# State-space step sizes from raw fp32 weights, in four quarters of a bank

## What is computed

```
proj = h @ w_in                                   # ..., dt_raw: 32 columns, ...
dt = softplus(dt_raw + dt_bias)                   # (tokens, 32)
a = -exp(a_log)
acs = cumsum(dt * a)                              # within each chunk of tokens
y_t = sum over s <= t of (C_t . B_s) exp(acs_t - acs_s) dt_s x_s
```

## Time and profile before

| | |
|---|---|
| median of 3 runs | 1696.14 us (1695.81 to 1696.51) |
| the profiled execution's own time | 1696.76 us |
| its span | 1694.7 us |
| TensorE busy | 1682.7 us, 99% of the span |
| VectorE, ScalarE, POOL busy | 874.8, 706.2, 792.7 us |
| mean granted TensorE clock | 0.998 of full speed |
| share of the chain that ended last | TensorE 97% |

### The profile page before, as it was taken

How to read it: one execution, slowest core, us unless ns; L and a number is a source line. 1 busy time by engine, 2 the same in 40 slices (tenths; PEclk the granted TensorE clock), 3 DMA queues, 4 the chain that set the end, 5 groups by cost and what they waited for, 6 DMA issues and landing times.

```text
span 1694.7 us, 21862 instructions
## 1 busy us (share of the span) xinstructions
PE 1682.7 (99%) x7957; PEld 1371.5 (81%) x7957; DVE 874.8 (52%) x1365; ACT 706.2 (42%) x977; POOL 792.7 (47%) x605
## 2 busy tenths in 40 slices
PE   9999999999999999999999999999999999999998
PEld 7777778788888888788878888788888888888887
DVE  6334474563616167797897878863355511101113
ACT  5333354431323134456464554784424422222232
POOL 1433354445545455543434344444545544654453
PEclk9999999999999999999999999999999999999999
DMA  5222222274636342233222332222222222332232
GB/s 187 91 84 74 74 96 90 75 261 161 229 118 216 124 155 99 96 106 125 100 100 101 118 103 99 100 75 100 75 99 100 76 98 99 129 128 91 99 124 100
DMA packets 32539, 193.82 MB, mean 114 GB/s; under 512 B 3648, under 2 KB 5696, under 8 KB 13792
## 3 DMA queue, kind: packets, MB, share of 16 engines
q1 hardware_dynamic: 25376, 158.89, 26.8%
q10 hardware_dynamic: 7104, 34.15, 6.0%
HBM read 190.86 MB, written 2.16 MB: 114 GB/s over the span
## 4 chain that ended last, share of the span: by engine, by line
PE 97%; DVE 1%; POOL 1%; DMA 1%; ACT 0%; SPq 0%; issue 0%; DVEq 0%; POOLq 0%
PE gemm_bank L511 25%; PE gemm_bank L504 25%; PE gemm_bank L505 25%; PE gemm_bank L542 4%; PE gemm_bank L558 4%; PE gemm_bank L551 3%; PE gemm_bank L546 1%; PE gemm_bank L789 1%; PE aux_bank L975 1%; PE aux_bank L655 1%; PE aux_bank L980 1%; PE aux_bank L960 1%; POOL h L482 1%; PE aux_bank L681 1%; DMA w_raw<-weights_dram 1%; PE aux_bank L672 1%
## 5 line engine op out<-in xcount | busy, mean ns | idle before, releaser
L454 POOL TENSOR_TENSOR w_lo<-w_raw,w_hi 128x512 fp32r<-128x512 f32 x580 | 771.2, 1361 | 881.8 <-ACT w_hi L1259 870.6
L504 PE MATMUL gemm_bank<-a_hi,w_hi 128*128 128x512 f32 x1008 | 402.6, 399 | 0.0
L505 PE MATMUL gemm_bank<-a_lo,w_hi 128*128 128x512 f32 x1008 | 393.2, 390 | 0.0
L1259 ACT ACTIVATE w_hi<-w_raw 128x2048 fp32r<-128x2048 f32 x145 | 276.5, 1907 | 187.0 <-PE gemm_bank L511 122.7
L504 PE MATMUL gemm_bank<-b_hi,w_hi 128*128 128x512 f32 x688 | 267.8, 389 | 0.0
L505 PE MATMUL gemm_bank<-b_lo,w_hi 128*128 128x512 f32 x688 | 267.6, 389 | 0.0
L511 PE MATMUL gemm_bank<-a_hi,w_lo 128*128 128x512 f32 x1024 | 258.6, 395 | 0.0
L511 PEld LDWEIGHTS gemm_bank<-a_hi,w_lo 128*128 128x128 f32 x1024 | 190.2, 188 | 44.9 <-issue 6.2
L504 PEld LDWEIGHTS gemm_bank<-a_hi,w_hi 128*128 128x128 f32 x1008 | 189.3, 188 | 43.9 <-issue 5.6
L505 PEld LDWEIGHTS gemm_bank<-a_lo,w_hi 128*128 128x128 f32 x1008 | 189.5, 188 | 39.4 <-issue 1.9
L2161 DVE SCALAR_TENSOR_TENSOR aux_bank<-scratch,gcol,aux_bank 128x511 f32<-128x511 f32 (+15 forms) x240 | 165.8, 734 | 14.2 <-ACT aux_bank L1485 11.9
(11 more groups left out here) (414 smaller groups left out, 2127.7 us busy)
## 6 DMA issues: line engine op xcount, KB each, us to landing
w_raw<-weights_dram SPq DMA_DIRECT2D x146, 1024.0 KB, 4.8
arena<-ada_dram ACTq DMA_DIRECT2D x32, 768.0 KB, 4.4
acc<-cum_rows ACTq DMA_DIRECT2D x8, 512.0 KB, 3.9
h<-x_t_dram SPq DMA_DIRECT2D x8, 256.0 KB, 6.2
row_b<-cum_rows ACTq DMA_DIRECT2D x4, 512.0 KB, 4.8
scratch<-cum_rows ACTq DMA_DIRECT2D x4, 512.0 KB, 4.3
out_t_dram<-a_raw SPq DMA_DIRECT2D x7, 256.0 KB, 2.2
w_raw<-weights_dram SPq DMA_DIRECT2D x4, 256.0 KB, 5.3
```

The source lines that it names most:

```text
L454: ins = pool.tensor_tensor(wlo[s][:, w], raw[s][:, w], whi[s][:, w].bitcast(F32), ALU.subtract)
L504: pe.matmul(gemm_bank[bank][:, :], whi[slot][:, w], hi[:, k, :], start=(n == 0), stop=False)
L505: pe.matmul(gemm_bank[bank][:, :], whi[slot][:, w], lo[:, k, :], start=False, stop=False)
L1259: act.activation(whi[panel % 2][:, :], raw[panel % 2][:, :], ACT.Copy).then_inc(w_hi_ready, 1)
```

## The change

The dt tile is no longer made of three rounded products per chunk. POOL copies the 32 columns of each chunk of the raw panel to `w_dt`. TensorE multiplies them as fp32, 128 x 32 weights by 512 columns, on a_hi and on a_lo, both read as fp32. Four chunks go to four quarters of the bank (partitions 0 to 31, 32 to 63, ...): chunks 0 to 3 after the a_hi chunk 3, chunks 4 to 7 after the a_hi chunk 7, and likewise on a_lo. So each quarter holds the sum over two chunks. The bias is added in the first quarter (it is zero elsewhere), and `dt_x` has 128 partitions. `turn_steps` multiplies it by `head_sum`, a 128 x 32 matrix of four identities below one another that POOL makes from `ident`; this adds the quarters and turns them at once. The pair's products on a_hi and a_lo are as before.

`turn_steps` is moved behind the high products of tile 2 of the group, and the low products of tiles 2 and 3 follow the high ones of both. ScalarE rounds panel P_DT + 2 right after the a_hi chunks, instead of after the dt tile; it waits for a signal on the last filler, the last reader of the panel buffer `whi[0]`.

```diff
@@ -168,7 +168,7 @@
         seg_pair = scratch[:, 14:16, :]
         ln_sum = b_n
         x_win = [seg_pair[:, 0, :], seg_pair[:, 1, :], state[:, 2, :]]
-        dt_x = scratch[0:SSM_HEADS, 4, :]
+        dt_x = scratch[:, 4, :]
         dt_e, dt_s, dt_q = [scratch[:, 2, c * P:(c + 1) * P] for c in range(3)]
         dt_r, dt_p = [aux[3][:, c * P:(c + 1) * P] for c in range(1, 3)]
         da_t = scratch[:, 3, 0:P]
@@ -194,6 +194,8 @@
         shift_out = new_part[:, 0:2]
         rinv2 = sb("rinv2", [P, QT])
         one_gain2 = sb("one_gain2", [P, 2])
+        head_sum = sb("head_sum", [P, 2 * SSM_HEADS])
+        w_dt = arena[:, 26, 0:KC * SSM_HEADS].rearrange("p (k n) -> p k n", k=KC)
         group_inv = sb("group_inv", [P, GROUPS * QT])
         group_root = sb("group_root", [P, GROUPS * QT])
         sq = sb("sq", [P, 2, S])
@@ -301,6 +303,8 @@
         cum_stored = sem("cum_stored")
         row_loaded = [sem(f"row_loaded{s}") for s in range(3)]
         dtt_done = sem("dtt_done")
+        dt_prepared = sem("dt_prepared")
+        wide_done = sem("wide_done")
         cumt_ready = sem("cumt_ready")
         last_done = sem("last_done")
         cross_step = sem("cross_step")
@@ -473,6 +477,14 @@
             pool.wait_ge(a_lo_ready, 3 * KC)
             low_parts(P_MLP // 2, 1, (1, 2, 3))
             panels_of(P_MLP // 2 + 1, P_DT // 2)
+            pool.wait_ge(w_loaded[0], 16 * (P_DT // 2) + 16)
+            pool.tensor_copy(w_dt[:, :, :], raw[0][:, :].rearrange("p (k n) -> p k n", k=KC)[:, :, 0:SSM_HEADS]) \
+                .then_inc(dt_prepared, 1)
+            pool.tensor_tensor(head_sum[:, :], ident[:, 0:2 * SSM_HEADS], ident[:, 2 * SSM_HEADS:4 * SSM_HEADS], ALU.add) \
+                .then_inc(dt_prepared, 1)
+            pool.wait_ge(dt_prepared, 2)
+            pool.tensor_tensor(head_sum[:, 0:SSM_HEADS], head_sum[:, 0:SSM_HEADS], head_sum[:, SSM_HEADS:2 * SSM_HEADS],
+                               ALU.add).then_inc(dt_prepared, 1)
             low_parts(P_DT // 2, 0)
             low_parts(P_DT // 2, 1, (0, 1), (first_half, 1))
             pool.wait_ge(w_hi_ready, P_GRP + 1)
@@ -878,39 +890,58 @@
                                start=True, stop=True)
             mm.then_inc(r_ready, 1)
 
+            def dt_products(operand, chunks, start=False, stop=False):
+
+                for g, k in enumerate(chunks):
+                    mm = pe.matmul(gemm_bank[T_DT % 4][g * SSM_HEADS:(g + 1) * SSM_HEADS, :],
+                                   w_dt[:, k, :], operand[:, k, :].bitcast(F32), start=start, stop=stop)
+                return mm
+
             def first_three():
 
-                three = [(P_DT, T_DT, 0), (P_GRP, T_GRP, 0), (P_GRP, T_GRP + 1, 1)]
+                pair = [(T_GRP + j, j) for j in range(2)]
                 for k in range(KC):
                     pe.wait_ge(a_hi_ready, 3 * KC + k + 1)
-                    for panel, t, j in three:
+                    for t, j in pair:
                         w = slice((2 * k + j) * P, (2 * k + j + 1) * P)
                         if k == 0:
-                            pe.wait_ge(w_hi_ready, panel + 1)
+                            pe.wait_ge(w_hi_ready, P_GRP + 1)
                             pe.wait_ge(bank_free[t % 4], t // 4 + 1)
-                        pe.matmul(gemm_bank[t % 4][:, :], whi[panel % 2][:, w], a_hi[:, k, :], start=(k == 0), stop=False)
+                        pe.matmul(gemm_bank[t % 4][:, :], whi[P_GRP % 2][:, w], a_hi[:, k, :], start=(k == 0), stop=False)
                         if k == 0:
-                            pe.wait_ge(w_lo_ready, panel + 1)
-                        pe.matmul(gemm_bank[t % 4][:, :], wlo[panel % 2][:, w], a_hi[:, k, :], start=False, stop=False)
-                for tiles in (three[:1], three[1:]):
-                    for k in range(KC):
-                        pe.wait_ge(a_lo_ready, 3 * KC + k + 1)
-                        for panel, t, j in tiles:
-                            w = slice((2 * k + j) * P, (2 * k + j + 1) * P)
-                            mm = pe.matmul(gemm_bank[t % 4][:, :], whi[panel % 2][:, w], a_lo[:, k, :],
-                                           start=False, stop=(k == KC - 1))
-                            if k == KC - 1:
-                                mm.then_inc(tile_done, 1)
-
-            keep_wide(7)
+                            pe.wait_ge(w_lo_ready, P_GRP + 1)
+                        pe.matmul(gemm_bank[t % 4][:, :], wlo[P_GRP % 2][:, w], a_hi[:, k, :], start=False, stop=False)
+                    if k == 3:
+                        pe.wait_ge(dt_prepared, 1)
+                        pe.wait_ge(bank_free[T_DT % 4], T_DT // 4 + 1)
+                    if k % 4 == 3:
+                        dt_products(a_hi, range(k - 3, k + 1), start=(k == 3))
+                for k in range(KC):
+                    pe.wait_ge(a_lo_ready, 3 * KC + k + 1)
+                    if k == 3:
+                        dt_products(a_lo, range(0, 4))
+                    if k == KC - 1:
+                        dt_products(a_lo, range(4, KC), stop=True).then_inc(tile_done, 1)
+                    for t, j in pair:
+                        w = slice((2 * k + j) * P, (2 * k + j + 1) * P)
+                        mm = pe.matmul(gemm_bank[t % 4][:, :], whi[P_GRP % 2][:, w], a_lo[:, k, :],
+                                       start=False, stop=(k == KC - 1))
+                        if k == KC - 1:
+                            mm.then_inc(tile_done, 1)
+
+            keep_wide(6)
+            pe.matmul(gemm_bank[MIX_SPARE][:, :], whi[P_DT % 2][:, 0:P], whi[P_DT % 2][:, 0:S], start=True, stop=True) \
+                .then_inc(wide_done, 1)
             first_three()
             ident_h = ident[0:SSM_HEADS, 0:SSM_HEADS]
 
             def turn_steps():
 
                 pe.wait_ge(bank_free[T_DT % 4], free_value(T_DT))
+                pe.wait_ge(dt_prepared, 3)
                 for c in range(QT):
-                    pe.transpose(aux[2][:, c * SSM_HEADS:(c + 1) * SSM_HEADS], dt_x[:, c * P:(c + 1) * P], ident_h)
+                    pe.matmul(aux[2][:, c * SSM_HEADS:(c + 1) * SSM_HEADS], dt_x[:, c * P:(c + 1) * P],
+                              head_sum[:, 0:SSM_HEADS], start=True, stop=True)
                 pe.wait_ge(decay_ready, 1)
                 pe.matmul(aux[3][:, 0:SSM_HEADS], neg_exp_a[:, 0:1].to_broadcast([SSM_HEADS, P]), ident_h,
                           start=True, stop=True).then_inc(dtt_done, 1)
@@ -982,8 +1013,13 @@
                     mm.then_inc(y_done, 2)
 
                 if first:
-                    turn_steps()
-                    g(2), g(3)
+                    blocks = [[(2 * k + j, k) for k in range(KC)] for j in range(2)]
+                    for j in range(2):
+                        tile_high(0, P_GRP + 1, T_GRP + 2 + j, 8, 16, blocks[j], a_hi, a_lo, first=(j == 0))
+                        if j == 0:
+                            turn_steps()
+                    for j in range(2):
+                        tile_low(0, P_GRP + 1, T_GRP + 2 + j, 8, blocks[j], a_hi, first=(j == 0))
                     running_sums()
                 else:
                     g(0), g(1), g(2), g(3)
@@ -1441,14 +1477,14 @@
 
             act.wait_ge(mod_ready, MLP_GROUPS)
             operand_shifted(2, 0)
+            act.wait_ge(wide_done, 1)
+            round_weights(0, P_DT + 2, 0, 0, 0)
 
 
             act.activation(neg_exp_a[:, :], cols[0:SSM_HEADS, COLS["a_log"]:COLS["a_log"] + 1], ACT.Exp) \
                 .then_inc(decay_ready, 1)
             act.wait_ge(tile_done, T_DT + 1)
-            act.activation(dt_x, gemm_bank[T_DT % 4][0:SSM_HEADS, :], ACT.Identity,
-                           bias=cols[0:SSM_HEADS, COLS["dt_bias"]:COLS["dt_bias"] + 1]).then_inc(bank_free[T_DT % 4], 1)
-            round_weights(0, P_DT + 2, 0, T_DT + 1, 0)
+            act.activation(dt_x, gemm_bank[T_DT % 4][:, :], ACT.Identity, bias=col("dt_bias", 0)).then_inc(bank_free[T_DT % 4], 1)
 
             def exp_steps():
                 act.wait_ge(dtt_done, 1)
```

## The result

| | before | after |
|---|---|---|
| median | 1696.14 us (1695.76 to 1696.84, 22 runs) | 1698.61 us (1698.12 to 1699.00, 22 runs) |
| span of the profiled execution | 1694.7 us | 1696.8 us |

The changed kernel takes 1.0014 times as long, with a 95% interval of 1.0008 to 1.0020: 2.5 us more, inside what was set beforehand as no difference (0.2%), though its interval leaves out 1. 5.44 us of TensorE's products were taken out, yet the kernel got longer.

A forecast was written before the change was run, and what follows sets the result against it. TensorE, busy 1682.7 of 1694.7 us, was taken as the bound. Terms -5.44 + 4.88 + 1.2 + 0.6 + 0.85, less 0.75 of old waits, gave +1.3; with +0.6 behind the stage, +1.9: 1698.0 us, range 1695.0 to 1702.3.

The forecast's parts named there:

- the likeliest case: Whole kernel: the forecast itself, 1697 to 1699.4 us, likeliest 1698.0; chance 0.54.
- step 6: Behind the stage: softplus chain starts 5.0 us later, DVE 2.4 late relative to TensorE, +0.6 us of new waits.
- 1 and 2: Stage: the dt tile's 24 products removed, 5.44 us; four fp32 visits of 1.22 us added, 4.88.
- A: Visits: the quarters run one behind another, 2.55 us more in each visit, giving 1707.4 us; chance 0.08.
- B: Visits: each quarter waits for its neighbour's second record, +1.27 us a visit, giving 1702.2 us; chance 0.05.
- 3: Products on a_hi: TensorE now waits for chunks 1 to 3, 1.2 us that the removed products had covered.
- 4: Next panel rounded sooner: POOL's subtractions stretch three a_lo to 1.7 us each; TensorE waits 0.85 us, bounds 0 to 2.
- 5: Turning of dt: 1.27 us plus 0.1 on return, +0.6 net; its waits are covered by the tile ahead.
- Rival C: First group: DVE becomes the bound, its lateness passing 1.8 to 2.2 us of slack, giving 1700.7 us; chance 0.08.
- D: Cheap case: subtractions don't hold a_lo, switching half hidden, DVE makes its deadlines; about -0.2, 1695.9 us; chance 0.22.
- E: Thin stream between 680 and 685: clock falls to half again, losing 1.7 us, giving 1699.7; chance 0.03.

The follow-up runs named there:

- one_quarter: Changed kernel with all dt products sent to one quarter of the columns, one behind another: 1709.01 us, ratio 1.0076 to the kernel before.
- filled: both_waits with panel 58 rounded ahead of the a_hi chunks, tile 2 as third tile beside each chunk, its a_lo products ahead of the turning: 1696.42 us.
- turn_first: Changed kernel with the turning back ahead of the group's tiles 2 and 3, each tile's low products behind its own high ones: 1697.87 us.
- copies_sooner: Changed kernel with VectorE copying the first group's head columns ahead of its first short convolution instead of behind it: 1697.19 us.
- both_waits: Changed kernel with POOL starting panel 58's low parts only after the last a_lo, and head columns copied ahead of the first short convolution: 1696.80 us.
- best: filled with the four visits to the quarters merged to two and the turning right behind the pair: 1695.86 us, ratio 0.9997 to the kernel before.

## Why the prediction was right, and where not

The time came out at 1698.61, 0.6 us over the 1698.0 and within the likeliest case. Steps 1 to 5 held as mechanisms and nearly as sizes; step 6 came near by luck in part, as told there. By the prediction's steps:

1 and 2, products and visits: right. A visit was put at 1.22 with its switches; from the start at 684.10 to the return of the full pace at 685.76, less two full products of 0.23, it is 1.20. The first records of all four quarters start between 684.43 and 684.45, the second ones from 684.88 to 684.90, as the prediction's sign of being right asked. Rivals A and B are refuted: all eight records of a visit end within 1.06 us, where B needs five times 0.43, and one_quarter shows what A's serial order costs (3.55 us). The weight loads of the first visit, in the same trace:

```profile
684.42 0.16 PEld L896 LDWEIGHTS gemm_bank<-a_hi,arena 128*32 128x32 f32 x8 [0.37 <-issue]
```

The Trainium skill ("TensorE: Matmul & The Clock Gate", Part 3: Packing small matmuls) says that weight loads overlap running products only where the row group differs. These rows don't bear it out: the products take all 128 rows, and all eight loads are over by 684.58, while the second records start at 684.88 only. The same page ("Why this matters for your kernels") says that products on separate column groups run at the same time, and the rows of after agree with that for fp32 and four groups.

3, the supply of a_hi: right. Chunk 3 was to be ready 3.89 us after the first product; it came at 683.28, 3.89 after. The filled kernel got 0.62 of this stage's waits back, so they were real.

4, the rounding moved ahead: mechanism right. Three a_lo were to take 1.7 us each and the last to end 16.15 after the first product; it ended at 695.53, 16.14 after. TensorE's wait was 0.58 and not 0.85, because it came to the last visit 0.2 later than walked through. Taking the clash out gave back 0.60. That rounding sooner gains nothing on TensorE was not tested, and the rows speak against it. In its old place the rounding stands behind dt_x, and the dt tile now ends later: dt_x ended at 697.41 in after, so with its 1.90 us the rounding would have ended at 699.3 at the soonest (an estimate from these two rows), and TensorE asked for the panel at 697.15. So the early rounding cost 0.6 in the clash, and may have saved some 2 us.

5, the turning: right, 1.27 against 1.24 (700.79 to 702.03). Uncovered by a tile ahead it was to lose 0.8; turn_first, which uncovers it, loses 0.44.

Sum to the running sums: +1.3 predicted, +1.22 measured.

6, VectorE's lateness: this is the step that was mis-sized. It had +0.6 in two waits "near 740 and 761"; measured is one wait of +1.41 at 740.61, and none at 762. Two errors stood against each other, and that the sum came near is in part their doing: without the clash the time would have been some 1.0 over before, as in copies_sooner, where +1.9 was forecast. The first error is the lateness relative to TensorE, 1.96 and not 2.4, which alone would have cost nothing. The second is that the prediction took back the 0.9 of a step that no longer meets POOL, but did not ask what VectorE would newly meet when it is late. The rows for it stood in the trace of before: the four copies of 0.17 us, and POOL's next burst 0.79 us behind their end. So did the price of such a meeting, in one more copy, of 98 columns, which takes 0.20 us at its other places and 0.85 at the first, inside POOL's burst:

```profile
L2166 DVE COPY gcol<-cols x4: 199/202/852, 705.3 to 998.7; 128x98 f32<-128x98 f32 x2, 128x98 f32 x2
```

(This row gives the shortest, the median and the longest of the four in ns.) Rival C had the right place and the right direction, a deadline missed past 2.2 us of slack. The measured wait of 1.41 lies between the 0.6 of the forecast and C's 3.3.

D failed on all its three conditions: a_lo did meet POOL, a visit cost its 1.20 in full, and VectorE missed a deadline. E is refuted. The window over the thin stream in after (columns as in the earlier trace rows) shows the clock granted in full, 1.00 of 2.4 GHz.

```profile
679.40:684.40 5.00, 4.72 (x16) 2.69 (x16) 5.00 (x9) 2.75 (x4) 5.00 (x5) 1.00 0.25 103
```

Where the 5.44 us went, then: four visits took 4.8, the uncovered a_hi supply and the bigger turning ate what was left and 0.6 more, a_lo's clash 0.6, and the copies' clash 1.4. The last two are accidents of order, and both_waits removes them. The first three are the change itself, which without accidents is still 0.59 us longer than before in the trace and 0.57 in the medians, though the interval of both_waits includes no difference. Only new work in the opened gaps (filled) and fewer visits (best) bring it level.

## What to carry to other kernels

Products taken off TensorE count only where its operands are already there; where a supply paces it, removing work opens gaps, and one must bring other work to stand in them. When a step makes an engine later, compare its new times with the bursts of the engine whose port it shares, down to its smallest instructions: slack computed from its own work alone is too large. Measuring from an event in the stage instead of from the start of the execution lets one trace account for tenths of a microsecond.

## What the runs showed of the hardware

Four fp32 products of 32 weight columns and 512 columns of data, in four column quarters, take nearly the time of one: 0.99 us to the next start, 1.85 for eight, and 3.55 for four in one quarter, 0.89 each. Two switches can be read beside that: 0.10 going into the narrow form (684.10 to 684.43, where a full product takes 0.23), and 0.11 between the first full product behind it and the second (685.42 to 685.76).

A copy of 128x32 fp32 from SBUF to SBUF takes 0.17 us alone, and up to 1.27 beside POOL in after. The stretched ones end at 726.15 and 727.43, where POOL's first two of four subtractions end too (its x4 from 724.82 to 729.91 steps by 1.27); behind each of them the next copy slips through in 0.17. The Trainium skill ("SBUF — State Buffer", Who interferes with whom) says that VectorE and GpSimd hold a shared pair of ports for a whole instruction, the other blocking, and that copies can take this pair; the ends of these copies agree. VectorE's convolution steps, which read one operand from PSUM, were not touched: 2.70 us for four, inside the same burst (the row at 727.55), as in this row of after outside it:

```profile
732.38 2.68 DVE L2197 SCALAR_TENSOR_TENSOR aux_bank<-scratch,gcol,aux_bank 128x503 f32<-128x503 f32 x4
```

So a short copy from SBUF to SBUF is the wrong thing to leave beside POOL, and its length in a quiet trace says nothing of its price.
